# Opening of a two-stage sequence model on one core: the convolution's gate half as eight fp32 sums by channel tiles, the norm token-major

## What is computed

```python
shift, scale, gate = split(silu(c) @ w_ada_mix + b_ada_mix, 3)
h = rms_norm(x, norm_mix_w) * (1 + scale) + shift
proj = h @ w_in                      # 1024 -> 9248 columns
conv_in, z, xbc, dt_raw, g_conv, g_ssm = split(proj)
a_half, b_half = split(conv_in, 2)   # 1024 columns each
u = a_half * sigmoid(b_half)         # then a causal convolution, a LayerNorm, ...
xbc = silu(causal_depthwise_conv(xbc, ssm_conv_w, ssm_conv_b))   # 3072 columns
...
shift, scale, gate = split(silu(c) @ w_ada_ffn + b_ada_ffn, 3)   # used later
```

## Time and profile before

| | us |
|---|---|
| median of three runs (lowest, highest) | 1455.03 (1454.02, 1457.22) |
| the profiled execution, its own time | 1460.29 |
| its span in the trace | 1458.0 |
| PE busy in it | 1377.9 (95%) |
| DVE busy | 1013.4 (70%) |
| ACT busy | 775.5 (53%) |
| first product of conv_b | 42.51 after the span's start |
| last product of conv_a | about 96.6 after the span's start |

### The profile page before, as it was taken

One profiled execution on the slowest core, in us unless ns is written; L12 is line 12 of the kernel. 1 busy time (PEld: TensorE's weight loads), 2 busy tenths in 40 slices (PEclk: granted clock), 3 DMA queues, 4 the chain that ended last, 5 costly groups with the idle time before them and its releaser, 6 DMA issues.

```text
span 1458.0 us, 26968 instructions
## 1 busy us (share of the span) xinstructions
PE 1377.9 (95%) x10935; PEld 1339.1 (92%) x10935; DVE 1013.4 (70%) x1792; ACT 775.5 (53%) x1221; POOL 395.3 (27%) x344
## 2 busy tenths in 40 slices
PE   4899998999999999999998899999999998999997
PEld 4899997989999999999888789999998997999996
DVE  5878898857577765689476568965466566986444
ACT  3534564577364433566763446664355744766343
POOL 1047784411610000039471401750007000320000
PEclk9899999999999999999999999999999999999998
DMA  9965663323656644747310014555554311465540
GB/s 351 377 218 184 189 208 102 100 87 131 199 193 236 225 150 160 213 119 200 103 43 1 0 30 145 174 188 189 180 169 140 122 59 59 146 201 189 187 145 29
DMA packets 202488, 223.86 MB, mean 154 GB/s; under 512 B 7608, under 2 KB 197723, under 8 KB 200317
## 3 DMA queue, kind: packets, MB, share of 16 engines
q1 hardware_dynamic: 201072, 220.67, 47.0%
q10 hardware_dynamic: 1293, 1.47, 0.3%
HBM read 221.07 MB, written 1.05 MB: 152 GB/s over the span
## 4 chain that ended last, share of the span: by engine, by line
PE 74%; DVE 14%; ACT 6%; issue 3%; POOL 2%; DMA 1%; SPq 0%; ACTq 0%; DVEq 0%; POOLq 0%
PE acc L631 18%; PE acc L635 18%; PE acc L632 18%; DVE GB L2034 3%; DVE pm L2020 2%; PE acc L732 1%; DVE wlo L494 1%; DVE ADA2B L1870 1%; ACT whi L484 1%; DMA XIN<-in_x 1%; PE acc L578 1%; PE acc L579 1%; POOL AM L1346 1%; PE acc L739 1%; PE acc L585 1%
## 5 line engine op out<-in xcount | busy, mean ns | idle before, releaser
L484 ACT ACTIVATE whi<-raw 128x1024 fp32r<-128x1024 f32 (+2 forms) x380 | 381.0, 1030 | 205.9 <-PE acc L635 194.0
L494 DVE TENSOR_TENSOR wlo<-raw,whi 128x1024 fp32r<-128x1024 f32 (+2 forms) x288 | 336.6, 1197 | 160.6 <-ACT whi L484 157.6
L494 POOL TENSOR_TENSOR wlo<-raw,whi 128x1024 fp32r<-128x1024 f32 x92 | 230.3, 2523 | 753.2 <-ACT whi L484 660.5
L631 PE MATMUL acc<-HH,whi 128*128 128x256 f32 x1664 | 415.9, 287 | 2.2 <-DVE XBC L2034 2.2
L632 PE MATMUL acc<-HL,whi 128*128 128x256 f32 x1664 | 411.8, 285 | 0.0
L631 PEld LDWEIGHTS acc<-HH,whi 128*128 128x128 f32 x1664 | 319.5, 192 | 6.8 <-issue 4.3
L632 PEld LDWEIGHTS acc<-HL,whi 128*128 128x128 f32 x1664 | 319.5, 192 | 0.3 <-issue 0.2
L635 PE MATMUL acc<-HH,wlo 128*128 128x256 f32 x1664 | 234.1, 284 | 0.3 <-POOL wlo L494 0.3
L635 PEld LDWEIGHTS acc<-HH,wlo 128*128 128x128 f32 x1664 | 214.5, 190 | 0.7 <-POOL wlo L494 0.6
L631 PE MATMUL acc<-HIDH,whi 128*128 128x256 f32 x688 | 170.0, 284 | 1.9 <-issue 1.0
L632 PE MATMUL acc<-HIDL,whi 128*128 128x256 f32 x688 | 169.2, 283 | 0.0
(11 more groups left out here) (573 smaller groups left out, 2434.6 us busy)
## 6 DMA issues: line engine op xcount, KB each, us to landing
raw<-in_mlp_w SPq DMA_DIRECT2D x64, 1024.0 KB, 5.2
raw<-in_w_in SPq DMA_DIRECT2D x36, 1024.0 KB, 5.4
raw<-in_w_ffn_in SPq DMA_DIRECT2D x22, 1024.0 KB, 5.4
raw<-in_a_w_in SPq DMA_DIRECT2D x16, 1024.0 KB, 5.8
raw<-in_b_w_in SPq DMA_DIRECT2D x12, 1024.0 KB, 5.3
ADR<-in_w_ada_ffn SPq DMA_DIRECT2D x8, 1024.0 KB, 9.2
raw<-in_w_ssm_out SPq DMA_DIRECT2D x8, 1024.0 KB, 5.0
raw<-in_w_ffn_down SPq DMA_DIRECT2D x8, 768.0 KB, 4.3
```

Source lines behind the costliest of these rows:

```text
L484: act.activation(whi[:, (s.t0 + 2 * u + h) % 4, 0:k], raw[:, place(s, b, u) % 4, 0:k, h * P:h * P + P], ACT.Copy).then_inc(hi_ready, 1)
L494: v.tensor_tensor(wlo[:, slot, 0:k], raw[:, place(s, b, u) % 4, 0:k, h * P:h * P + P], whi[:, slot, 0:k].bitcast(F32), ALU.subtract).then_ ...
L631: pe.matmul(acc[:, q, 0:T], whi[:, slot, i], hh, start=first and i == 0, stop=False)
```

## The change

The section conv_b is gone. Its product is computed in full float32, without rounding or rests: for each of the eight channel tiles k of `h` a *slab*, 128 rows by 1024 columns of `w_in` (0.5 MB), is loaded into a slot of `raw`, and eight matmuls add `slab_k` times `h_k` to eight sums in the four banks of `acc`. That can start as soon as the first channel tile of `h` exists, so the modulation is computed by pairs of channel tiles: `w_ada_mix` comes in eight *pieces* of 1 MB, two for each pair (256 columns of shift and of scale, half the rows each), DVE multiplies each in four steps of 512 columns, PE sums four columns, DVE makes the pair's shift and scale, ACT writes `h_k` (into `ACC`) and `HH`, and DVE takes `HL` as their difference. The norm is taken with the tokens on the partitions: ACT squares the rows of `x` with a running sum, and the turn of `x` is repeated as a matmul with a diagonal matrix `RD` of the inverse roots, into `H`.

SP's order is now x, then for each pair two pieces and two slabs; slab 4 and those after it wait until the product four before has been done, and everything behind them on SP waits too. Two of the eight slices of `w_ada_ffn` stand ahead of slab 7, the six others (`late`) between the blocks of conv_a. The six small loads follow slab 7. `small_tok` now follows the fp32 products, with conv_a behind it.

```diff
-            for n in range(4):
-                load_ada(n)
             sp.dma_start(XIN[:], a["x"][0].rearrange("(t p) d -> p t d", p=P)).then_inc(x_in, 16)
-            for n in range(4, 7):
-                load_ada(n)
+            for g in range(NP // 2):
+                for i in (2 * g, 2 * g + 1):
+                    load_piece(i)
+                load_slab(2 * g)
+                if g == 3:
+                    for i in range(2):
+                        load_late(i)
+                load_slab(2 * g + 1)
...
+            def load_slab(i):
+                if i >= 4:
+                    sp.wait_ge(k_used, i - 3)
+                sp.dma_start(raw_slab(i), w_in[i * P:i * P + P, D:D + SLAB]).then_inc(landed[i % 4], 16)
...
+            for tk in range(NT):
+                ins = act.activation(ACC[:, 4 * tk:4 * tk + 4].rearrange("p k t -> p (k t)"), XIN[:, tk], ACT.Square,
+                                     accum_out=XS[:, 0, tk:tk + 1])
...
+            xr_copy(2)
+            xr_copy(3)
+            rows_in(range(6, len(pieces)))
...
+            for k in range(KT):
+                if k == 0:
+                    act.wait_ge(xc_ok, 8)
+                act.wait_ge(mod_ok, k // 2 + 1)
+                g_, s_ = MOD[:, 8 + k:9 + k], MOD[:, k:k + 1]
+                act.activation(ACC[:, k], H[:, k], ACT.Identity, scale=g_, bias=s_).then_inc(h_ok, 1)
+                act.activation(HH[:, k], H[:, k], ACT.Identity, scale=g_, bias=s_).then_inc(n_hh, 1)
...
+            ffn_late(0)
+            for k in (6, 7):
+                first_lo(k)
+            ffn_late(1)
+            v.wait_ge(par_t, 2)
+            v.tensor_copy(par[:, 512:NPAR], pm[:, 2, 0:NPAR - 512])
+            ffn_late(2)
...
             softplus(0)
+            ffn_late(6)
             log_decays()
+            ffn_late(7)
...
+            first_sums(0)
+            for k in range(KT):
+                pe.wait_ge(landed[k % 4], 16 * (k // 4 + 1))
+                pe.wait_ge(h_ok, k + 1)
+                for i in range(8):
+                    if i == 5 and k % 2 and k < KT - 1:
+                        first_sums(k // 2 + 1)
+                    m = first_product(k, i)
...
+                if k == 1:
+                    par_turn(0, 4)
+                elif k == 5:
+                    par_turn(4, NPT)
```

More of the change, by code:

```diff
@@ L134, in program @@
     SEC = {s.name: s for s in SECS}
-    for k in ("conv_b", "conv_a", "xbc", "z", "g", "conv_out", "ssm_out", "w_out", "ffn_in", "ffn_down", "a_qkv", "mlp1_0",
+    for k in ("conv_a", "xbc", "z", "g", "conv_out", "ssm_out", "w_out", "ffn_in", "ffn_down", "a_qkv", "mlp1_0",
               "mlp2_0", "mlp1_1", "mlp2_1"):
@@ L169, in program @@
         s.hi_ahead = True
[L170 to L178, removed]
+        s.lo_done = s.ahead or s.name in ("conv_a", "conv_out", "ffn_in")
     def place(s, b, u):
@@ L1403, in small_hi, with xr_copy @@
+            def xr_copy(q):
+                act.wait_ge(xr_p, q + 1)
+                act.activation(H[:, 2 * q:2 * q + 2], xr_bank(q).rearrange("p (d t) -> p d t", d=2), ACT.Copy).then_inc(xc_ok, 1)
+            x_copy(0)
+            x_copy(1)
+            xr_copy(0)
+            x_copy(2)
+            xr_copy(1)
+            x_copy(3)
+            xr_copy(2)
+            xr_copy(3)
+            rows_in(range(6, len(pieces)))
             def small_hi(n, w_):
                 act.activation(WSH[n][:], w_[:], ACT.Copy).then_inc(wsh_ok, 1)
-            def conv_b_hi():
-                for h in range(2):
-                    split_hi(act, SEC["conv_b"], 0, 0, h)
@@ L1421, in a_more @@
+            act.wait_ge(dt_in, 16 * 6)
+            small_hi(0, ws1)
+            for h in range(2):
+                split_hi(act, SEC["conv_a"], 0, 0, h)
+            for q in range(4):
+                act.wait_ge(k_used, KT - 1 + 2 * q + 2)
+                act.activation(G[:, 2 * q:2 * q + 2], acc[:, q].rearrange("p (d t) -> p d t", d=2), ACT.Sigmoid)\
+                   .then_inc(acc_free, 2)
             def a_more(b):
@@ L2057, in _ @@
                           extra=xbc_more)
-            for n8 in range(ADA_SIDE, 20):
-                ada_rest(n8 - 8)
+            for i in range(4):
+                mix_gate(i)
                 taps(24)
@@ L2575, in ada_sums @@
-            def ada_sums(n, src, done, i0=0):
-                for i in range(i0, i0 + n):
+            pe.wait_ge(n_std, STDS["mix"])
+            for q in range(4):
+                if q == 3:
+                    pe.wait_ge(xc_ok, 1)
+                for i in range(4):
+                    d_, tk = 2 * q + i // 2, i % 2
+                    m = pe.matmul(xr_bank(q)[:, i * P:i * P + P], XIN[:, tk, d_ * P:d_ * P + P], RD[:, tk], start=True, stop=True)
+                m.then_inc(xr_p, 1)
+            pe.wait_ge(masks, 2)
@@ new lines, in par_turn, with first_product @@
+            def par_turn(i0, i1):
+                pe.wait_ge(par_in, 16 * (len(pieces) - 3))
+                for i in range(i0, i1):
+                    n = min(P, NPAR - P * i)
+                    m = pe.transpose(pm[:, 2, (i - i0) * P:(i - i0) * P + n], PRW[0:n, i, :], ident[0:n, 0:n])
+                m.then_inc(par_t, 1)
+            def first_product(k, i):
+                return pe.matmul(acc[:, i // 2, i % 2 * T:i % 2 * T + T], raw_slab(k)[:, i * P:i * P + P], ACC[:, k],
+                                 start=k == 0 and i % 2 == 0, stop=k == KT - 1, skip_group_check=True)
@@ L2588, in h_parts @@
                         lambda k: pe.wait_ge(n_hl, 8 * HN[name] + k + 1))
-            pe_section(pe, SEC["conv_b"], hrhs, ready=h_parts("mix"))
             def small_tok(n, done):
```

359 lines of the change are left out of this document (188 added, 171 removed).

## The result

| kernel | median, us (runs) | ratio to the kernel before, 95% interval | DVE takes conv_a's last tile at, us |
|---|---|---|---|
| before | 1455.51 (10) | 1 | 96.66 |
| the changed kernel | 1461.57 (10) | 1.0033 [1.0021, 1.0046] | 94.19 |
| the same again, measured later, beside the first experiments | 1463.18 (6) | 1.0053 [1.0037, 1.0070] | 94.14 |

The account below looks back on a forecast made before the run. PE was taken to bound the kernel, busy 95% of the span. Conv_a's earlier end (-1.8), the stop in xbc (+4.6) and the slow restart (+1.75) sum to +4.5 us: 1459.5 on the median of 1455.0, range 1448 to 1466.

Parts of the forecast that it names:

- Start: First fp32 product on PE at 24.4 us (23.3 to 25.5), with 17 `PRW` load starts holding ACT 6.8 us before `h_0`.
- the first rival: The 17 starts don't hold ACT: first product at 17.6, 1452.8 us, or 1449.5 with the short stop; chance 0.15.
- Products: The 64 fp32 matmuls on PE all end at 57.8 us, with 2.5 lost to a slow clock at their beginning.
- The wait for `WSX`: Ahead of `small_tok`, PE waits 5.0 us (3 to 7) for dt's weight rests behind slice 2; `small_tok` then takes 6.9.
- Conv_a's end: Conv_a ends at 94.8 us against 96.6 before, a gain of 1.8 us (from -1 to 5).
- The stop in xbc: Ahead of xbc's tile 4, PE stops 4.6 us (3.3 to 6.7) for DVE, delayed by two slices; slow restart adds 1.75.
- Behind this nothing changes … so the loss stays.: After xbc, PE and then DVE's chain of taps follow xbc's end as before, so the +4.5 us reaches the end.
- Starts that don't hold ACT: Rival at ACT's 17 `PRW` starts: first product at 17.6, 1452.8 us, or 1449.5 with the short stop; chance 0.15.
- no stop in xbc: Rival: PE meets no stop in xbc, so only conv_a's end counts: 1453.2 us; chance 0.13.
- an early slice 2: Rival: slice 2 lands early enough, PE goes on at 57.8 with a fast `small_tok`: 1452.0 us; chance 0.08.
- slow products: Rival: PE stays at 1.2 GHz through the fp32 products, 27 us more for 64 matmuls: 1479 us; chance 0.05.

Follow-up runs that it names:

- slices_early: Changed kernel with ffn slices 3 and 4 ahead of conv_a's first tile, 5 to 7 behind its blocks 0 to 2, none behind conv_a: 1456.14 us, 1.0002.
- keep_busy: Changed kernel with 39 throwaway matmuls on PE between the last fp32 product and the wait for `WSX`: 1460.31 us, 1.0033.
- late_z: Changed kernel with 14 throwaway matmuls (1.7 us) on PE behind block 0 of section z, near 184 us: 1458.51 us, 1.0033.
- rows_behind: Changed kernel with the 17 starts of `PRW` loads behind the second channel tile of `h` on ACT instead of ahead of the first: 1456.71 us, 1.0007.
- rows_rests: Changed kernel with the `PRW` starts behind `h`'s second tile and dt's weight rests (`WSX`) formed ahead of slice 2: 1447.78 us, 0.9952.
- slices_xbc: rows_rests with the last two ffn slices (6 and 7) loaded and added up inside xbc: 1443.45 us, 0.9918.
- turns_later: slices_xbc with the turns of the parameter rows behind products 3 and 6 instead of 1 and 5, DVE's copy one pair later: 1441.47 us, 0.9910.

## Why the prediction was right, point by point

- **Start.** 24.4 was forecast and 24.53 measured, but two terms were off and made each other up, which is luck. silu(c) came at 8.25 and not 5.5, since PE's first turn waited to 7.97 for the row of `norm_mix_w`, and the scaled turns began at 13.27 where 9.9 was forecast; PE then made them in some 3.9 us at full clock where 5.5 to 7.0 with a slow clock was taken. The same start lay at 26.1 to 26.4 in three other traces (slices_early, keep_busy, late_z), outside the forecast's 23.3 to 25.5. The term that mattered was right: the 17 starts took 6.5 us (17.15 to 23.69) where 6.8 was read from the earlier trace rows, and moving them behind `h` was worth 4.9 to 6.5 us of the program (rows_behind). The sentence of the Trainium skill (DMA: Bandwidth & Descriptors, "Issuing engines are not separate DMA queues") compares one start with its own transfer. One start by itself agrees with it: they took 0.26 to 0.45 us each, for pieces of 0.5 to 64 KB, and in rows_behind the last piece, started at 24.77 in 0.35 us, let PE go on only at 31.08. What cost was that 17 of them stood in a row on an engine that had to compute next, so the first rival didn't follow from that sentence.
- **Products.** All ended at 57.85, forecast 57.8; the slow beginning cost 1.9 (7.70 less 5.78 for 26 records), forecast 2.5. It isn't there in each execution: rows_rests, slices_xbc and turns_later began at full clock (5.85 for the same 26).
- **The wait for `WSX`.** Slice 2 reached DVE at 59.81, forecast 59.7; the wait was 4.79, forecast 5.0; the small products took 6.8, forecast 6.9. keep_busy confirms that these were slow for the idle time, not for themselves. The price of the small loads (1.5) was too low, since the six held SP for 7.6 us (43.06 to 50.63), but the DMA engines were full all that time (share 1.00 to 1.11 from 38 to 50 us), so slice 2 came no later. Conv_a's end: the forecast's 94.8 against DVE's last tile at 94.19, a gain of 2.5 where 1.8 was forecast.
- **The stop in xbc.** 4.12 and, in the second trace, 5.76 (forecast 4.6, 3.3 to 6.7). One meeting with POOL of 1.3 was counted; both slices met it, and took 3.82 and 3.21 instead of 2.35, 2.3 us in all. What the forecast missed is that its base already held a meeting: softplus's product of 2.21 stood in the 10.1 us that DVE needed before. In the first trace that product took 0.50 and so paid for most of the slices' meetings; in the second it took 2.05, and this is the difference between 4.12 and 5.76. Behind the stop tile 4 took 4.44 (109.80 to 114.24) instead of 2.88, 1.56 lost, forecast 1.75. The durations on DVE agree with the rule of the Trainium skill (SBUF — State Buffer, "Who interferes with whom") that a DVE instruction with two SBUF inputs and a POOL instruction that reads SBUF exclude each other; POOL was splitting but for 0.9 us of that time.
- **"Behind this nothing changes … so the loss stays."** The loss does stay: DVE began `ADA2B` at 173.89 before and at 178.25 and 179.89 now, 4.4 and 6.0 later (forecast 4.5), and at 230 us it is 6.0 with the long wait in both traces and 6.7 with the short one in both. But DVE's steps and PE's wait there aren't fixed, in either kernel. The forecast read the wait of 4.25 from one trace as if every execution had it, and of the two short executions among the ten the one that was traced is of the other kind.
- **Rivals.** Starts that don't hold ACT, no stop in xbc, an early slice 2 and slow products are all excluded by the first trace: 6.04 of idle ACT, waits of 4.12 and 4.79, and 5.78 for 26 records.

## What to carry to other kernels

DMA starts on an engine's queue hold that engine's own work up (17 of them 6.5 us here): put them where it waits, and look again when what it waited for comes earlier. When an opening is pulled forward, list what stood between on each in-order engine only because there was time: here small loads, a slice ahead of `WSX` and two slices ahead of xbc cost 5 to 10 us each by the single edits, and together hid all that the rebuilt opening gained. Once such waits were out of the way the transfers came next: moving the use of two slices forward gave 2.0 us, within the intervals, and moving their loads past the stretch some 4 by the medians.

## What the runs showed of the hardware that was not expected

A PE that is held up for a moment can gain more at a later wait than it lost; before's second trace won 4.2 us in this way. In nine traces with a moment of low clock between 160 and 182 us, and in the two with throwaway matmuls there, DVE's steps of `ADA2B` ran into POOL's splits less often (read from their durations): a pair takes 2.59 to 2.62 without a meeting (late_z) and took 4.61 and 5.23 with one or two (the changed kernel's second trace). PE's wait of 4.25 us near 230 us then became 0.3. A single trace of each kernel can so show the wrong sign, as the first pair did here (spans of 1458.0 before, 1455.0 after).

Two traces of the kernel before differ by 7.1 us (1458.0 and 1450.9). 2.1 of these stand already at the first step of `ADA2B` (173.89 and 171.80), and 4.2 come with the wait and the slow clock behind it. The second trace lost some 2.4 again up to 715 us, and the first some 3 near 1124 us, where its clock was 0.61 and 0.53 from 1120 to 1128 and the second's was 1.00. The clock of such stretches isn't the same in each execution of one kernel, so differences of 1 to 3 us between single traces say little here.
